# Hybrid encoder step: second-head copies of attention on VectorE, with moves in three phases

## The reference, cut to what matters

```python
def token_mixer(h, st, ...):
    c = split_cols(h @ w_in + b_in)                       # the projection
    ...
    conv_out, conv_buf = causal_conv(qk_pre, s_conv, conv_w, conv_b)   # 4 taps
    conv_out = jax.nn.silu(conv_out)
    qb = conv_out[..., :W_B]                              # mLSTM queries
    kb = conv_out[..., W_B:] * DH_B ** -0.5               # mLSTM keys, scaled
    ...
    S_a, oa = scan_stream(gla_block, ...)                 # recurrent, chunk by chunk
    (C_b, n_b, m_b), hb = scan_stream(mlstm_block, ...)
    ...
    yc = dsa_prompt(q_c, qi, wi, ...)                     # attention over the best 256 keys
    return y, (k_new, v_new, ki_new, S_a, C_b, n_b, m_b, conv_buf)

def dsa_attend(...):
    iscore = ...relu(qi . ki)...; _, sel = lax.top_k(iscore, n_sel)
    logits = jnp.einsum('btkgd,btnkd->btkgn', q, k_sel) * DH_C ** -0.5
    p = jax.nn.softmax(where(valid, logits, -inf), axis=-1)
    o = jnp.einsum('btkgn,btnkd->btkgd', p, v_sel)
```

## Time and profile before

| what | value |
|---|---|
| three runs | 1385.22, 1391.04, 1391.98 us; median 1391.04 |
| the profiled execution | 1385.14 us, of which the trace's span 1383.3 us |
| busy share of the span | PE 87%, DVE 49%, ACT 32%, POOL 30% |
| PE busy | 1201.9 us in 5971 instructions |
| mean granted TensorE clock | 0.90 of full speed |
| chain that ended last | reaches back to 1028 us only: PE L2166 13%, PE L2190 6% |

### The profile page before, as it was taken

The page is one execution under the profiler, slowest core; times in us unless marked ns, Lnnn a source line. Parts: engine busy times, 40 slices in busy tenths (PEclk is TensorE's granted clock), DMA queues, the critical chain, the costliest instruction groups (busy, mean ns, idle before and its releaser), DMA issues. The chain is left out here.

```text
span 1383.3 us, 18207 instructions
## 1 busy us (share of the span) xinstructions
PE 1201.9 (87%) x5971; PEld 663.8 (48%) x5972; DVE 681.0 (49%) x1861; ACT 447.5 (32%) x845; POOL 419.6 (30%) x469
## 2 busy tenths in 40 slices
PE   4899999999998268896978899999839999999990
PEld 3455655455554146684655584555533333333330
DVE  7115699999992055524645522222561322222227
ACT  6224100211111322203666531111315444444417
POOL 0001021106388522105876005442111333333210
PEclk9999899999999557766999999999759999999995
DMA  9300000011010200004000004532714798968445
GB/s 369 144 16 1 1 1 1 0 31 31 31 45 0 65 0 1 1 3 153 1 1 2 1 1 175 193 135 95 273 31 143 208 280 292 330 208 273 87 132 204
DMA packets 35774, 136.92 MB, mean 99 GB/s; under 512 B 9658, under 2 KB 12266, under 8 KB 30842
## 3 DMA queue, kind: packets, MB, share of 16 engines
q1 hardware_dynamic: 28218, 108.79, 21.2%
q0 software_dynamic: 7488, 27.27, 8.4%
HBM read 101.24 MB, written 34.80 MB: 98 GB/s over the span
## 5 line engine op out<-in xcount | busy, mean ns | idle before, releaser
L439 PE MATMUL p<-hT,p_wfm 128*128 128x512 f32 (+1 forms) x624 | 207.4, 495 | 2.1 <-PEq L106 2.1
L2166 PE MATMUL p_G<-p_wgu,p_xT 128*64 x416 | 186.2, 601 | 0.4 <-ACT p_xT L2091 0.4
L2168 PE MATMUL p_G<-p_high_gu,p_xT 128*64 128x512 f32 x416 | 186.2, 601 | 0.0
L453 PE MATMUL p<-p_wtm,hT 128*128 128x399 f32 (+1 forms) x480 | 165.6, 504 | 0.0
L439 PEld LDWEIGHTS p<-hT,p_wfm 128*128 128x128 f32 x624 | 105.7, 192 | 104.1 <-issue 104.1
L453 PEld LDWEIGHTS p<-p_wtm,hT 128*128 128x128 f32 (+1 forms) x480 | 85.6, 180 | 77.4 <-issue 14.6
L1987 POOL DMA_INDIRECT sum_rows<-p_ys,p_dest_of x26 | 55.4, 2131 | 199.1 <-DVE p_ys L2028 199.1
L2101 ACT COPY p_high_gu<-p_wgu 128x1024 f32 x104 | 101.0, 1042 | 39.8 <-issue 36.8
L583 DVE TENSOR_SCALAR_CACHE_REDUCE key_bias<-p_score,p_trial 128x272 bf16<-128x272 f32 (+4 forms) x155 | 108.4, 759 | 1.1
L1367 DVE CUSTOM_DVE_ANT_0 p_logit<-p_L,key_bias 128x272 f32<-128x272 f32 (+6 forms) x120 | 56.9, 500 | 105.2 <-PE p_L L1435 81.0
L2166 PEld LDWEIGHTS p_G<-p_wgu,p_xT 128*64 128x64 f32 x416 | 55.3, 138 | 110.5 <-issue 110.5
(11 more groups left out here) (454 smaller groups left out, 2075.3 us busy)
## 6 DMA issues: line engine op xcount, KB each, us to landing
p_wgu<-in_w_gu SPq DMA_DIRECT2D x16, 2048.0 KB, 9.4
p_wd<-in_w_down SPq DMA_DIRECT2D x16, 1024.0 KB, 12.3
p_wfm<-in_w_fm SPq DMA_DIRECT2D x13, 512.0 KB, 3.7
p_wtm<-in_w_tm SPq DMA_DIRECT2D x8, 598.5 KB, 15.7
p_x<-in_x SPq DMA_DIRECT2D x9, 512.0 KB, 9.4
h_rows<-p_x SPq DMA_DIRECT2D x9, 512.0 KB, 14.8
p_h<-h_rows SPq DMA_DIRECT2D x9, 512.0 KB, 3.3
h_rows<-p_h SPq DMA_DIRECT2D x9, 512.0 KB, 2.7
```

The costliest lines, as they stand in the source:

```text
L439: mm = nc.tensor.matmul(ps[3 * u + c][:, 0:b - a], w[:, u, k, :], m.hT[:, k, a:b], start=k == 0, stop=k == KD - 1)
L453: mm = nc.tensor.matmul(bank["tokens", n][0:rows, 0:TG], stream, m.wtm[:, k, g * TG:(g + 1) * TG], start=k == 0, stop=k == KD - 1)
L2166: nc.tensor.matmul(pG[u][low, :], xT[:, u, k, low], wgu[:, ds(slot, 1), k, :].rearrange("p a n -> p (a n)"), start=k == 0, stop=k == KD - 1)
L2168: mm = nc.tensor.matmul(pG[u][high, :], xT[:, u, k, high], high_gu[:, u, k, :], start=k == 0, stop=k == KD - 1)
```

## The change

The edits, part by part:

- `phase_project`: ScalarE copies tile 6 before the SiLU of channel 0, tiles 7 and 8 before that of channel 1, 9 and 10 before channel 2, 11 and 12 before channel 3. The scaling of the two key tiles moves from GpSimd to the end of VectorE's list. SP writes the rows of v once the token tiles are complete, ahead of the convolution's rows; the rows of k and kidx (six DMAs) move to the start of `phase_recurrent`, which waits for them at its end.
- `phase_recurrent`: `operands(t + 2)` moves from behind `output(t)` into `totals(t)`, between the multiplication and the wait for `num_ready`. `s_c` and `s_n` move to the start of `phase_dsa`, as two DMAs each.
- `phase_dsa`: VectorE copies the turned groups of each pair's second head, after `output(p - 3)`; ScalarE copies those of the first, between its two exponentials. The semaphore `pT_copied` becomes `first_copied` and `second_copied`. Both engines wait for the state DMAs before the first copy into the buffer `pT1`, which lies over the old states.

```diff
+def rows_to(sp, m, d, name, landed):
+
+    c, width = {"k": (CK, 128), "v": (CV, 128), "kidx": (CI, DI)}[name]
+    out = d["p_" + name]
+    sp.dma_start(out[0:META, :], m.tm[0:META, MT, c:c + width]).then_inc(landed, 16)
+    sp.dma_start(out[META:PROMPT, :].rearrange("(j p) c -> p j c", p=P), m.tm[:, 0:NT, c:c + width]).then_inc(landed, 16)
+    sp.dma_start(d["s_" + name], m.tm[:, SAMPLE, c:c + width]).then_inc(landed, 16)
 
...
+                sp.wait_ge(bias_added, len(groups))
+                rows_to(sp, m, d, "v", m.rows_out)
                 sp.wait_ge(acc_ready, 4)
                 sp.dma_start(d["p_conv"].rearrange("c p j -> p c j"), last_p[:, :, :]).then_inc(conv_out, 16)
                 sp.dma_start(d["s_conv"].rearrange("c p i j -> p c i j"), last_s[:, :, :, :]).then_inc(conv_out, 16)
                 sp.wait_ge(conv_out, 32)
-                sp.wait_ge(bias_added, len(groups))
-                sp.wait_ge(rows_copied, TT + 1)
-                n = 0
-                for name, c, width in (("k", CK, 128), ("v", CV, 128), ("kidx", CI, DI)):
-                    out = d["p_" + name]
-                    sp.dma_start(out[0:META, :], m.tm[0:META, MT, c:c + width]).then_inc(rows_out, 16)
-                    sp.dma_start(out[META:PROMPT, :].rearrange("(j p) c -> p j c", p=P),
-                                   m.tm[:, 0:NT, c:c + width]).then_inc(rows_out, 16)
-                    sp.dma_start(d["s_" + name], m.tm[:, SAMPLE, c:c + width]).then_inc(rows_out, 16)
-                    n += 3
-                sp.wait_ge(rows_out, 16 * n)
...
-                for c in range(2):
-                    pool.wait_ge(silu_ready, 3 + c)
-                    g.tensor_scalar(m.fm[:, F_BK + c, :], m.fm[:, F_BK + c, :], DHB ** -0.5, None, ALU.mult).then_inc(keys_scaled, 1)
...
                 for c in range(4):
-                    for u in range(2 if c < 3 else 1):
-                        feature_tile(F_BK // 2 + c, u)
+                    for k in range(F_BK + max(2 * c - 1, 0), F_BK + 2 * c + 1):
+                        feature_tile(k // 2, k % 2)
                     act.wait_ge(acc_ready, c + 1)
                     nc.scalar.activation(m.fm[:, F_BQ + c, :], acc[:, :], ACT.Silu).then_inc(silu_ready, 1)
...
+                for c in range(2):
+                    dve.wait_ge(silu_ready, 3 + c)
+                    nc.vector.tensor_scalar(m.fm[:, F_BK + c, :], m.fm[:, F_BK + c, :], DHB ** -0.5, None, ALU.mult).then_inc(keys_scaled, 1)
...
+                rows_to(sp, m, d, "k", m.rows_out)
+                rows_to(sp, m, d, "kidx", m.rows_out)
...
                 sp.wait_ge(g_done, 1)
                 put(d["s_gla"].rearrange("h k i v -> (h k) i v"), S0[:, :, :])
-                sp.wait_ge(m_done, 1)
-                sp.wait_ge(n_copied, 1)
-                for p, e in every_two:
-                    put(d["s_c"][2 * p + e, :, :, :], C0[m_rows(e), p, :, 0:DVA])
-                    put(d["s_n"][2 * p + e, :, :], nlast[m_rows(e), p, :])
                 sp.wait_ge(out, 16 * n)
+                sp.wait_ge(m.rows_out, 16 * 9)
...
                                       over(by_parity(arg[:, 1, slot(t), :]).unsqueeze(3), [P, 2, 2, VE]), ALU.mult))
+                    if t + 2 < TT:
+                        operands(t + 2)
                     dve.wait_ge(num_ready, t + 1)
...
                     output(t)
-                    if t + 2 < TT:
-                        operands(t + 2)
...
+                for p in range(2):
+                    sp.dma_start(d["s_c"][2 * p:2 * p + 2, :, :, :].rearrange("e k i v -> (e k) i v"), m.C0[:, p, :, 0:DVA]).then_inc(m.states_out, 16)
+                    sp.dma_start(d["s_n"][2 * p:2 * p + 2, :, :].rearrange("e k i -> (e k) i"), m.nlast[:, p, :]).then_inc(m.states_out, 16)
...
+                sp.wait_ge(m.states_out, 16 * 4)
...
+                def copies(g):
+                    t, h = heads[g]
+                    bl = blocks(t)
+                    p = g // 2
+                    if p >= 2:
+                        dve.wait_ge(o_ready, p - 1)
+                    if g == 3:
+                        dve.wait_ge(m.states_out, 16 * 4)
+                    for k in range(n_groups(t)):
+                        n = groups_to[g] + k
+                        dve.wait_ge(turned, n + 1)
+                        part = bl[4 * k:4 * k + 4]
+                        rows = max(x[1] for x in part)
+                        nc.vector.tensor_copy(pT[p % 2][0:rows, 4 * k:4 * k + len(part), 1, :],
+                                              pP[n % 2][0:rows, 0:len(part), :]).then_inc(second_copied, 1)
...
                     if p >= 3:
                         output(p - 3)
+                    if p:
+                        copies(2 * p - 1)
                 reciprocal(NP - 1)
+                copies(2 * NP - 1)
...
+                    if g == 2:
+                        act.wait_ge(m.states_out, 16 * 4)
...
-                        nc.scalar.copy(pT[p % 2][0:rows, 4 * k:4 * k + len(part), g % 2, :],
-                                       pP[n % 2][0:rows, 0:len(part), :]).then_inc(pT_copied, 1)
+                        nc.scalar.copy(pT[p % 2][0:rows, 4 * k:4 * k + len(part), 0, :],
+                                       pP[n % 2][0:rows, 0:len(part), :]).then_inc(first_copied, 1)
...
                             exponent(2 * p + i)
-                    for i in range(2):
-                        if p:
-                            copies(2 * p - 2 + i)
+                        if p and i == 0:
+                            copies(2 * p - 2)
...
-                            pe.wait_ge(pT_copied, n - 1)
+                            of = max(x for x in range(g + 1) if groups_to[x] <= n - 2)
+                            pe.wait_ge((first_copied, second_copied)[of % 2], copied_to[of // 2] + n - 2 - groups_to[of] + 1)
...
-                    pe.wait_ge(pT_copied, groups_to[2 * p + 2])
+                    pe.wait_ge(first_copied, copied_to[p + 1])
+                    pe.wait_ge(second_copied, copied_to[p + 1])
```

More of the change, by code:

```diff
@@ L151, in phase_norm_in @@
         m.wtm_in, m.normal_out = nc.alloc_semaphore("p2_wtm_in"), nc.alloc_semaphore("p2_normal_out")
+        m.rows_out = nc.alloc_semaphore("p4_rows_out")
         rows_of = lambda t: P if t < TT else META
@@ L638, in phase_recurrent @@
         sem = Semaphores(nc, "p4_")
+        sem.made += [m.rows_out]
         VE = DVA + 1
@@ L1227, in phase_dsa @@
         sem = Semaphores(nc, "p6_")
+        sem.made += [m.states_out]
         GQ = HC // KVC
@@ L1274, in phase_dsa @@
         n_groups = lambda t: -(-len(blocks(t)) // 4)
+        copied_to = [sum(n_groups(t) for t, h in heads[0:2 * p:2]) for p in range(NP + 1)]
         groups_to = [sum(n_groups(t) for t, h in heads[:g]) for g in range(len(heads) + 1)]
```

13 lines of the change are left out of this document (7 added, 6 removed).

## The result

The changed kernel takes 1328.97 us (median of 4 runs, 1327.67 to 1334.99), the kernel before 1388.13 us beside it (4 runs, 1384.54 to 1391.98): a ratio of 0.9578 (95% interval 0.9540 to 0.9617), 59 us or 4.2% less. The profiled execution was the slowest of the four, 1334.99 us (span 1333.2), against 1385.14 (1383.3). So the two traces explain 50 us of the 59. All runs of the changed kernel on record, the later set with a median of 1334.04 included, lie between 1327.64 and 1335.05.

A forecast was written before the change was run, and what follows sets the result against it. Phases end at barriers, each bound by what ends it: GpSimd's convolutions, waits at the scores, state DMAs, ScalarE's copies. Savings 19.5 + 8.8 + 7.0 + 9 = 44.3 from 1385.1 gave 1341 us, range 1328 to 1357.

The forecast's parts named there:

- rival 2: Recurrent loop: without its waits TensorE keeps the full clock, 12 us more saved, 1329 us in all; chance 0.12.
- A, project: Project phase: earlier SiLUs and convolutions, key scaling on VectorE and moved row DMAs save 19.5 us, bounds 17.5 and 20.5.
- rival 1: Project phase: VectorE's ties drag GpSimd's channel 2 to half speed, 8.0 us of the gain go, 1348.8; chance 0.13.
- B, operands: Recurrent loop: operands issued earlier in VectorE's idle time remove TensorE's waits at the scores, saving 8.8 us, bounds 5 and 10.
- the seven waits: Recurrent loop: TensorE's waits at the scores in seven turns, 8.8 us in all, were to vanish.
- C, states: Recurrent phase's tail: state DMAs moved to attention's start let the phase end 7.0 us sooner, bounds 4.8 and 7.2.
- D, attention: Attention: sharing copies between VectorE and ScalarE shortens TensorE's waits for them, saving 9 us, bounds 0 and 11.
- the row at 773.94: Attention: profile row where ScalarE was free and TensorE waited 0.58 us, taken as the wait left per waiting turn.
- Rivals 3 and 4: Attention: VectorE's copies late, no net saving there, 1349.8, chance 0.08; or copies make a serial ring, 1411, chance 0.02.

The follow-up runs named there:

- the later set: The changed kernel measured once more, unchanged, as the yardstick beside later kernels: median 1334.04 us over 6 runs, ratio 0.9608.
- The run with filled pauses: Eight useless 128 x 128 TensorE products ahead of each turn's wait for the scores' operands, added to the kernel before: 1375.72 us, ratio 0.9909.

## Why the prediction was right, and where it was off

The direction, the places and three of four sizes held; the whole came out 12 us (0.9%) too slow. The saving was 59 us (56 in the later set) against 44 forecast; 3 us of the difference are the base, since the forecast starts from 1385.1 and the median beside the changed kernel was 1388.1. The time lies within 1 us of the range's lower bound, and inside it only because that bound was put down to 1328 for rival 2: the forecast's own range was 1333 to 1349, which has the later median (1334.04) just in it and this one not. So the range held here through the rival, not through the sum.

- **A, project** (19.5; measured 19.1 in the profiled pair, 21.1 alone). The bound on channel 2 was 33.6 to 38.3 us, and the time was the lower end: the ties slowed GpSimd no more over 33.7 us than they had over 25.6. So rival 1 did not happen. VectorE's scaling was hidden, as told.
- **B, operands** (8.8; measured 17.7 in the profiled pair and 20.0 alone, 13 to 20 against all five executions with the pauses). This is the step that failed: "the seven waits vanish: 8.8". They did, and a full-clock turn fell by 1.16 us as foreseen, but the sum kept the mixture of clocks of before. The run with filled pauses shows that the mixture was itself made by the pauses. It was rival 2, priced at 12 us more (measured 9 to 11) and given 0.12. My argument against it, that turns at either clock had the same waits, was no evidence: the waits needn't differ for their removal to decide.
- **C, states** (7.0; measured 7.3, 5.9 alone). The states landed ahead of the first copy into `pT1`.
- **D, attention** (9; 5.8 in the profiled pair, 7.9 alone). The waits came down to a mean of 8.5/15 = 0.57 us, the 0.58 of the row at 773.94. The tail cost 2.0 where I had 0.8, as the pause there took the clock down too. The rest of the shortfall from 9 to 5.8 is a profiled execution before with an uncommonly short slow stretch at the start (12.4 us; the other five with the old attention had 20 to 21): a sum against one execution takes its luck with it. The mechanism was misread in one point: I took VectorE's help for the cause, but the order on ScalarE gives some two thirds of the gain and nearly all of that in the two-group tiles, for which the sum was made. Rivals 3 and 4, about VectorE's copies, did not happen; they help by some 2.8 us. Its copy of 512 elements took 0.69 us (0.58 to 0.61, plus 0.1, forecast).

The sum with B at 18 to 20 instead of 8.8 is 1330 to 1332, and the two medians of the changed kernel are 1328.97 and 1334.04.

## What to carry to other kernels

Where TensorE pauses in every turn of a loop and its granted clock is a mixture of two levels, count the wait twice: once as time, and once as what the loop would take at the full clock; the price of a turn at either level stands in the trace. Before work is given to a second engine, look whether the first engine only has it in the wrong place: an instruction that waits for a late input should not stand ahead of one that another engine waits for. And put GpSimd's long products where VectorE does nothing that reads two SBUF inputs.

## What the runs showed of the hardware

- TensorE's pauses of 0.6 to 1.5 us, one in each turn of 8 to 12 us, went with granted clocks of 0.70 to 0.80 over seven turns in five profiled executions; with useless products in their place it was 0.89 in one. With the pauses removed it was 0.88 to 0.94 in seven, and 1.00 in one without the second turn's stall as well. Where it was below 1.00, the turn with that stall or the first turn ran at the lower clock.
- A stretch in which TensorE was busy throughout could stay at 1.2 GHz as well: in the changed kernel some 27 us with the small products of the sample tile (32 rows, 64 columns), and attention's first 20.4 us. In the 3.4 us between the two, in which TensorE was busy for 0.40 us, the granted clock was 1.00:

```profile
562.00:587.00 25.00, 24.20 (x136) 19.68 (x137) 3.89 (x9) 0.37 (x1) 0.00 (x0) 0.50 0.00 0
587.00:590.40 3.40, 0.40 (x6) 0.18 (x3) 1.79 (x4) 0.22 (x1) 0.01 (x1) 1.00 0.20 77
590.41:610.80 20.39, 19.77 (x106) 12.35 (x108) 10.35 (x56) 7.76 (x30) 17.36 (x39) 0.50 0.71 246
```

- When the clock rose in attention differs by execution: 12.4 and 12.6 us into the phase in two (the kernel before, and that with GpSimd's product moved), 16.3 to 25.6 in the twelve others. Why stays open; it was not tried. By two with the same attention, the latter and the changed kernel beside it, 7.5 us of that are worth 3.4 us before the two-group tiles, more than the tail or VectorE's copies are worth.
- GpSimd's 3.6 us product held a 4-column VectorE instruction with two SBUF inputs for 2.37 us instead of 0.15, and left those that read PSUM alone.
- VectorE's copy out of PSUM took 0.69 us for 128 x 512, ScalarE's 0.58 to 0.59; the scaling of 128 x 1168 in SBUF took VectorE 0.77 to 0.95 us and GpSimd 3.16.
